# Final norm tile by tile behind the value joins, the gating join ahead of the residual's additions, and the recurrent output's spread one tile behind with two root buffers

## What is computed

```python
def rms_norm(x, g):                       # the first block's end: x = rms_norm(x, final_norm_g)
    y = xf * lax.rsqrt(jnp.mean(xf * xf, axis=-1, keepdims=True) + EPS)
    return y * g

def sgu_mixer(h, w_in, gain, w_s, b_s, w_out):
    u, v, z = jnp.split(h @ w_in, 3, axis=-1)
    u = gelu(u)
    v = rms_norm_2(gelu(v), gain)
    mixed = einsum('gpq,bcqgd->bcpgd', w_s, vc) + b_s
    return (u * mixed * silu(z)) @ w_out  # x = x + gate * this

def rwkv7_output(y, r, k_dir, v, z, r_k, ln_gain, ln_bias, w_out):
    mean = jnp.mean(yh, axis=-1, keepdims=True)                  # over each head's 64 columns
    var = jnp.mean(jnp.square(yh - mean), axis=-1, keepdims=True)
    yn = ((yh - mean) * lax.rsqrt(var + RWKV_LN_EPS)).reshape(y.shape) * ln_gain + ln_bias
    return ((yn + bonus) * silu(z)) @ w_out
```

## Time and profile before

| | |
|---|---|
| median of 3 runs | 4689.03 us (4688.02 to 4695.07) |
| profiled execution | 4691.61 us, its span 4689.6 us |
| TensorE busy | 4518.3 us, 96% of the span |
| VectorE, ScalarE, GpSimd busy | 41%, 24%, 21% |
| mean granted TensorE clock | 0.985 of full |
| chain that ended last | TensorE 89%, VectorE 6%, ScalarE 2%, issue 2% |

### The profile page before, as it was taken

One profiled execution on the slowest core, in us unless ns is written; L12 is line 12 of the kernel. 1 busy time (PEld: TensorE's weight loads), 2 busy tenths in 40 slices (PEclk: granted clock), 3 DMA queues, 4 the chain that ended last, 5 costly groups with the idle time before them and its releaser, 6 DMA issues.

```text
span 4689.6 us, 68532 instructions
## 1 busy us (share of the span) xinstructions
PE 4518.3 (96%) x29082; PEld 3061.3 (65%) x29082; DVE 1914.1 (41%) x3500; ACT 1116.1 (24%) x2249; POOL 998.9 (21%) x722
## 2 busy tenths in 40 slices
PE   9999999999999999999999989988999999999999
PEld 4446888544688887665555567776544555556888
DVE  3633452463355232224524258785201444421324
ACT  2141000113110022110423134443112333322220
POOL 1102443110244332323023000000000101003444
PEclk9999999998999999999999999999999999999999
DMA  3161222115122212111244332222111000012221
GB/s 130 54 225 63 90 95 86 47 63 216 63 90 95 86 36 72 54 54 46 105 139 151 111 86 66 81 79 101 65 69 38 30 15 30 29 54 72 95 80 69
DMA packets 115101, 378.72 MB, mean 81 GB/s; under 512 B 32752, under 2 KB 58480, under 8 KB 85360
## 3 DMA queue, kind: packets, MB, share of 16 engines
q1 hardware_dynamic: 103840, 332.92, 20.5%
q0 software_dynamic: 9808, 37.75, 2.4%
q10 hardware_dynamic: 1152, 3.67, 0.2%
HBM read 334.46 MB, written 39.85 MB: 80 GB/s over the span
## 4 chain that ended last, share of the span: by engine, by line
PE 89%; DVE 6%; ACT 2%; issue 2%; POOL 0%; DMA 0%; DVEq 0%; SPq 0%; ACTq 0%
PE ps L369 37%; PE ps L337 16%; PE ps L612 15%; PE ps L4190 2%; PE ps L2541 2%; PE ps L343 2%; PE ps L633 2%; PE ps L4109 1%; PE ps L1079 1%; PE ps L1035 1%; PE ps L4201 1%; PE ps L3195 1%; PE ps L4112 1%; PE ps L4108 1%; PE ps L4110 1%
## 5 line engine op out<-in xcount | busy, mean ns | idle before, releaser
L369 PE MATMUL ps<-A 128*128 128x256 f32 (+1 forms) x3568 | 872.0, 397 | 5.2 <-DVE A L1710 2.2
L369 PE MATMUL ps<-A,W 128*128 128x256 f32 (+1 forms) x3296 | 830.5, 405 | 5.5 <-DVE A L2398 3.1
L369 PEld LDWEIGHTS ps<-A 128*128 128x128 f32 x3568 | 676.0, 190 | 162.0 <-issue 8.5
L369 PEld LDWEIGHTS ps<-A,W 128*128 128x128 f32 x3296 | 624.6, 190 | 175.0 <-DVE A L2398 3.5
L612 PE MATMUL ps<-A,W 128*128 128x512 f32 (+1 forms) x1632 | 702.0, 585 | 2.8 <-DVE A L580 1.3
L612 PEld LDWEIGHTS ps<-A,W 128*128 128x128 f32 x1632 | 308.9, 192 | 358.4 <-issue 349.5
L337 PEld LDWEIGHTS ps<-A 64*64 64x64 f32 (+2 forms) x8032 | 379.3, 144 | 140.4 <-issue 79.2
L337 PE MATMUL ps<-A 64*64 64x64 f32 (+5 forms) x8032 | 429.7, 240 | 40.7 <-ACT A L3411 14.1
L337 PE MATMUL ps<-A,W 64*64 64x64 f32 (+3 forms) x2560 | 355.7, 322 | 8.3 <-ACT A L4356 5.8
L337 PEld LDWEIGHTS ps<-A,W 64*64 64x64 f32 (+2 forms) x2560 | 217.3, 156 | 138.7 <-issue 118.6
L440 POOL TENSOR_TENSOR A<-W 128x512 f32<-128x512 f32 (+2 forms) x88 | 133.0, 1512 | 425.8 <-PE ps L369 386.5
(11 more groups left out here) (449 smaller groups left out, 5533.2 us busy)
## 6 DMA issues: line engine op xcount, KB each, us to landing
W<-in_ada SPq DMA_DIRECT2D x48, 1024.0 KB, 5.3
W<-in_w_up SPq DMA_DIRECT2D x44, 1024.0 KB, 4.8
W<-in_w_in SPq DMA_DIRECT2D x18, 1024.0 KB, 4.8
W<-in_sgu_v SPq DMA_DIRECT2D x16, 1024.0 KB, 4.9
W<-in_sgu_u SPq DMA_DIRECT2D x16, 1024.0 KB, 4.9
W<-in_sgu_z SPq DMA_DIRECT2D x16, 1024.0 KB, 4.8
W<-in_sgu_o SPq DMA_DIRECT2D x16, 1024.0 KB, 4.8
W<-in_rw_in SPq DMA_DIRECT2D x16, 1024.0 KB, 5.1
```

Source lines behind the costliest of these rows:

```text
L369: t = e.matmul(ps, x(k), y(k), start=first and k == 0, stop=k == kt - 1, skip_group_check=True)
```

## The change

1. **Final norm.** `final_normed_dve` takes a tile number. The eight multiplications stand one each behind the joins of blocks (1, 1) to (3, 2), and the spread's bank is now always bank 5; the value blocks (1, 0) to (3, 2) of layer 0 take their banks from the other seven.
2. **Gating join.** For pair 0 of the SGU output (layers 0 and 3) the join 22, v = v + D, stands ahead of the additions of q to the residual.
3. **Recurrent output.** The root is one ScalarE instruction from PSUM with scale and bias, so that L3890 goes; it writes one of two buffers `b.rows`. P runs two tiles behind C and T four (before, one and three). The root stands ahead of the next square on ScalarE, whose table for roots is loaded before the stage. On VectorE bonus and z gate of a tile stand behind its own multiplication.
4. A spread of the MLA stage takes bank 4 in place of its turn in the ring.

```diff
-def final_normed_dve(pl, e):
-    S_, at = pl.S, ("rs", "final", SC)
+def final_normed_dve(pl, e, k):
+    S_, at, r = pl.S, ("rs", "final", SC), pl.R[:, k, SC:N]
     e.wait_ge(*S_.squares_summed.at(at))
-    for k in range(8):
-        r = pl.R[:, k, SC:N]
-        e.scalar_tensor_tensor(out=r, in0=r, scalar=vec(pl, "fg", k), in1=bank(pl, at)[:, 0:S], op0=ALU.mult,
-                               op1=ALU.mult).then_inc(*S_.normed.next(("final", k, SC), frees=at if k == 7 else None))
-    e.wait_ge(*S_.normed.last())
+    e.scalar_tensor_tensor(out=r, in0=r, scalar=vec(pl, "fg", k), in1=bank(pl, at)[:, 0:S], op0=ALU.mult,
+                           op1=ALU.mult).then_inc(*S_.normed.next(("final", k, SC), frees=at if k == 7 else None))
...
+        ring = "01234567" if i or c == 0 else "0123467"
...
-            final_spread_pe(pl, e, "final", (SC, S), 0, "latent")
+            final_spread_pe(pl, e, "final", (SC, S), 0, "latent", "5")
...
-            if (i, c, p) == (0, 1, 0):
-                final_normed_dve(pl, e)
+            if i == 0 and (c, p) > (1, 0):
+                final_normed_dve(pl, e, 3 * c + p - 4)
+    if i == 0:
+        e.wait_ge(*S_.normed.at("final", 7, SC))
...
-    add(0, b.half, q)
-    add(1, 0, q)
+    if p:
+        add(0, b.half, q)
+        add(1, 0, q)
     e.wait_ge(*S_.seventh.at(at, 7))
     e.wait_ge(*made.last())
     e.tensor_tensor(v, v, d, ALU.add).then_inc(*made.next((at, 22)))
+    if not p:
+        add(0, b.half, q)
+        add(1, 0, q)
...
-    for s in range(11):
+    for s in range(12):
         if s < 8:
             centred(s)
         if 0 <= s - 1 < 8:
             sums(s - 1)
-        if s >= 3:
-            taken_in(s - 3)
-        if 0 <= s - 1 < 8:
-            spread(s - 1)
+        if s >= 4:
+            taken_in(s - 4)
+        if 0 <= s - 2 < 8:
+            spread(s - 2)
...
 def output_act(pl, e):
+    e.activation(pl.root[:, 0:1], table(pl, "ones")[:, 0:1], ACT.Sqrt).then_inc(*S_.roots.next())
...
-        x = pl.root[:, 0:192]
-        e.wait_ge(*S_.mean_squares.at("rw_norm", k))
-        e.activation(x, x, ACT.Sqrt).then_inc(*S_.roots.next(("rw_norm", k)))
+        e.wait_ge(*S_.squares_summed.at(at))
+        if k >= 2:
+            e.wait_ge(*S_.squares_summed.at(("rw_rs", k - 2, 1)))
+        e.activation(b.rows[k % 2], bank(pl, at)[:, 0:192], ACT.Sqrt, bias=table(pl, "eps64"), scale=1.0 / 64).then_inc(
+            *S_.roots.next(at, frees=at))
...
+            x, at = b.rows[(s - 1) % 2], ("rw_norm", s - 1)
             e.wait_ge(*S_.roots.at(at))
             e.reciprocal(x, x).then_inc(*S_.inverse_roots.next(at))
+        if s < 2:
+            continue
+        k, y = s - 2, b.s_[:, s - 2, :]
+        for j, half in enumerate(b.halves):
+            at = ("rw_rs", k, j)
+            e.wait_ge(*S_.squares_summed.at(at))
+            e.scalar_tensor_tensor(out=y[:, half], in0=y[:, half], scalar=vec(pl, "lng", k), in1=bank(pl, at)[:, 0:384],
+                                   op0=ALU.mult, op1=ALU.mult).then_inc(*S_.out_normed.next(*([k] if j else []), frees=at))
+        e.wait_ge(*S_.out_normed.at(k))
+        e.wait_ge(*loads[k // 2].at("gates"))
+        e.scalar_tensor_tensor(out=y, in0=y, scalar=vec(pl, "lnb", k), in1=b.bo[:, k, :], op0=ALU.add,
+                               op1=ALU.add).then_inc(*S_.out_normed.next(("bonus", k)))
+        e.wait_ge(*S_.out_normed.at("bonus", k))
+        e.tensor_tensor(y, y, b.zz[:, k, :], ALU.mult).then_inc(*S_.z_gated.next(k))
```

More of the change, by code:

```diff
@@ L91, in constants @@
     out["sides"] = np.where(i % 32 < 16, EPS * D, EPS * EPS * D)[:, None]
+    out["eps64"] = np.full((P, 1), 64e-5)
     out["w16"] = np.stack([((i // 32) % 2 == k // 2) & (i % 2 == k % 2) for k in range(4)], 1)
@@ L216, in placed @@
     pl.MOD = ctx.enter_context(nc.sbuf_tensor("MOD", [P, 96, 2], F32))
-    pl.A_SIZE = 53202 - (8 * N + NSLOT * SLOT + n + NCOLS + 192 + 32)
+    pl.A_SIZE = 53203 - (8 * N + NSLOT * SLOT + n + NCOLS + 192 + 32)
     pl.A = ctx.enter_context(nc.sbuf_tensor("A", [P, pl.A_SIZE], F32))
@@ L2118, in values @@
         keys = {7: [("sgu_v", j, 2 * c)], 3: [("sgu_v", j, 2 * c + 1)]} if last else {}
-        return seven_pe(pl, e, at, sgu_tokens(b, p), halves_of(sgu_columns(pl, b, c), b.vt), 4, 256, "01234567", ready,
+        ring = "01234567" if i or c == 0 else "0123467"
+        return seven_pe(pl, e, at, sgu_tokens(b, p), halves_of(sgu_columns(pl, b, c), b.vt), 4, 256, ring, ready,
                         S_.first_kept.at(at), keys, bare=(i, c) == (0, 0), warmed=5 * ((i, c, p) == (3, 0, 0)))
@@ L3753, in lay_output @@
     b.s_, b.bo, b.zz = A(8, N), A(8, N), A(8, N)
+    b.rows = [A(N // 4) for _ in range(2)]
     b.x = lambda k, s: b.s_[:, k, s[0]:s[0] + s[1]]
@@ L3809, in spread @@
                     row = table(pl, "ident", o, o + 1).to_broadcast([P, 64])
-                    t = e.matmul(ps[half, 192 * c:192 * c + 192], row, pl.root[:, 0:192], start=True, stop=True)
+                    t = e.matmul(ps[half, 192 * c:192 * c + 192], row, b.rows[k % 2], start=True, stop=True)
             t.then_inc(*S_.squares_summed.next(at))
@@ L3858, in root @@
     def root(k):
[L3859 to L3861 removed]
+        at = ("rw_norm", k)
+        e.wait_ge(*S_.squares_summed.at(at))
[3 more added lines that the diff above has]
+            *S_.roots.next(at, frees=at))
     for s in range(9):
@@ L3869, in output_act @@
                     *S_.centred.next((s, j), frees=at))
-            e.wait_ge(*S_.centred.last())
+        if s:
+            root(s - 1)
+        if s < 8:
+            e.wait_ge(*S_.centred.at(s, 1))
             if s >= 2:
@@ L3873, in output_act @@
             e.activation(pl.sq[s % 2], b.s_[:, s, :], ACT.Square).then_inc(*S_.act_squares.next(("rw_norm", s)))
-        if s:
-            root(s - 1)
     end(pl, "output", "act")
@@ L3884, in output_dve @@
     for s in range(1, 10):
-        k, y = s - 1, b.s_[:, s - 1, :] if s < 9 else None
-        before = b.s_[:, s - 2, :] if s >= 2 else None
         if s < 9:
[L3888 to L3895, removed]
@@ L3896, in output_dve @@
-        if s < 9:
+            x, at = b.rows[(s - 1) % 2], ("rw_norm", s - 1)
             e.wait_ge(*S_.roots.at(at))
             e.reciprocal(x, x).then_inc(*S_.inverse_roots.next(at))
[L3899 to L3909, removed]
+        if s < 2:
+            continue
@@ L4036, in mla_pe @@
     features_pe(pl, e, "ml_cq", [("ml_cq", i) for i in range(3)], 8, 256, b.h, b.xseg, ring=wide, ready=ready, warmed=6,
-                beside=lambda m, seg: squares(m - 1) if m else spread_pe(pl, e, ("mod", 2), BOTH, order=BOTH[0:1]))
+                beside=lambda m, seg: squares(m - 1) if m else spread_pe(pl, e, ("mod", 2), BOTH, "4", order=BOTH[0:1]))
     features_pe(pl, e, "ml_ckv", ["ml_ckv"], 8, 256, b.h, b.segs, ring=wide, ready=ready,
```

## The result

The changed kernel takes 4674.83 us, the median of 7 runs (4665.76 to 4677.28); the kernel before took 4690.65 us on the same chip (7 runs, 4687.21 to 4699.22). The ratio is 0.996, with a 95% interval of 0.995 to 0.997: 15.8 us less, where 14.6 were forecast (4674.4, from the 4689.03 of the first three runs). The profiled execution took 4668.58 us, its span 4666.6 us, which is 6.3 us under the median, where the profile before stood 2.6 us above the median it was taken with.

The account below looks back on a forecast made before the run. TensorE, busy for 96% of the span, was taken as the bound, so only its waits and slow clock counted. 5.7 + 4.6 + 4.3 = 14.6 us off the median of 4689.03 gave 4674.4 us, range 4667 to 4682.

Parts of the forecast that it names:

- Final norm, 5.7 us forecast: SGU values, layer 0: a 4.05 us bank wait and its slow clock go, 6.98 us, less a new 1.3 us wait.
- the eighth tile's wait: Ahead of `sgu_u`: product 1 needs bank 5, which the norm's last tile frees, so TensorE newly waits 1.3 us.
- rival (d): SGU values: the norm wait was for VectorE and moves to the next join; first term -1.3, time 4681.4; chance 0.05.
- Rival (c): Value blocks: with seven banks, A waits for the block before's C; slower, time 4698; chance 0.05.
- its 1.1 us to spare: Value blocks: A takes the bank of the block before's C, whose freeing is hidden behind product 4 with 1.1 us over.
- Gating join, 4.6 us forecast: SGU output, layer 3: 3.09 us wait and 1.79 us slow clock go, less a 0.3 us wait for bank 0.
- Recurrent output, 4.3 us forecast: Gain at the stage's start: its end moves from 3297.7 to 3293.4, despite a new wait ahead of the fourth S.
- if the stage from the first C to the last T isn't 56 us: Recurrent output: the prediction's sign of being wrong; it expected 56 us, against 60.7 before.
- TensorE waits 4.0 us ... I take 2.3: Recurrent output, fourth S: z landing after 10.1 us delays the bonus; a 4.0 us wait plus 2.3 us slow clock.
- rival (a): Recurrent output: the bonus doesn't wait for its loads; third term 9.7 us, time 4669.0; chance 0.2.
- Rival (b): Clock falls ahead of `sgu_u` (2.9 us) and at recurrent output's start (3.7 us); gain 8.0, time 4681.0; chance 0.24.
- the third term: The recurrent output's gain, forecast at 4.3 us, between 0.6 and 9.7 us.

Follow-up runs that it names:

- x4_bank: Kernel before with only the final norm's bank choice and the MLA spread's bank 4, the eight multiplications left in one piece: 4686.43 us, ratio 0.9979.
- x2_join: Kernel before with only the gating join moved ahead of the additions of q: 4691.98 us, ratio 0.999.
- x8_first: Changed kernel with A's addition of pair 0 ahead of the two of q in the SGU output: 4672.82 us, ratio 0.9955 to the kernel before.
- x1_norm: Kernel before with only the final norm's single tiles and banks, and the MLA spread's bank 4: 4683.14 us against 4696.31, ratio 0.9973.
- after_again: The changed kernel run once more, nothing altered: 4671.67 us, ratio 0.9953 to the kernel before.
- x6_slab: Changed kernel with the first slab of output weights loaded behind tile 1's bonus and z too: 4672.23 us, ratio 0.9955 to the kernel before.
- x3_out: Kernel before with only the recurrent output's new order: 4686.99 us, ratio 0.9987.

## Why the prediction came out right, point by point

- **Final norm, 5.7 us forecast: 5.69.** The wait for a bank, its slow clock, the eighth tile's wait (1.3 forecast, 1.17 in the row, 1.44 in the stretch) and the kept clock behind it all held. `x4_bank` shows that the bank was the cause; rival (d) is wrong. Rival (c) is wrong too: a block takes 12.11 us. But the prediction's reading of the turns there, with its 1.1 us to spare, is wrong: a block takes four turns of seven, so A gets the bank of C of the block before the last, and it is D that gets the bank of the block before's A. In the profile after, ScalarE is done with A of block (1, 1) at 1720.06 and product 7 of block (1, 2) wants the bank at 1728.14: 8.1 us to spare. The rival was less likely than its working made it.
- **Gating join, 4.6 us forecast: 4.67.** `x2_join` shows it alone, `x8_first` that the 0.27 us left was bank 0. Of this term the slow clock's part (1.8) isn't the wait's fixed price: in `x1_norm` and `x4_bank` the same 3.09 us wait left the clock up, and the stretch at 49.03 us. Measured from there the edit is worth 2.98 us. That the term came out to 0.1 us is in part luck: the profile before was one of those in which the clock fell.
- **Recurrent output, 4.3 us forecast: 8.3.** This is the term that was mis-sized, and by the prediction's own sign ("if the stage from the first C to the last T isn't 56 us") it was wrong here: the stage took 52.46 us. TensorE's order of events was right to 0.1 us up to C4. Two figures of the step "TensorE waits 4.0 us ... I take 2.3" failed. z landed 8.5 us behind its issue in the place of 10.1, which made the wait 1.65 us shorter. The landing time of one execution had been carried over as if it were fixed, and that execution was the odd one: in the nine other profiles whose slab stands ahead of this z it took 8.2 to 8.9 us, in `x1_norm`, `x2_join` and `x4_bank` too, whose recurrent output is the old one. So the new order didn't make it sooner. Why it took 10.1 that once no run shows. And the clock didn't fall, 2.3 us more. 1.65 + 2.3 is the 4.0 that the term was short. In `after_again` it did fall, and the term was 6.35. So the truth lies between the forecast and rival (a): the mechanism of the forecast (the bonus waits), most of (a)'s gain. `x6_slab` is rival (a) made true: 50.29 us, 10.5 gained, where (a) had 9.7.
- **Rival (b)** doesn't hold as priced: the clock stayed up at the wait ahead of `sgu_u` in all seven profiles that have it, and at the start of the recurrent output of the five profiles with the third edit as the change has it, it fell in one (`after_again`), for 1.7 us and not 3.7.
- **The sum** came out nearer than its terms: 14.6 forecast, 18.7 in the two profiles' own stretches, 15.8 by the medians. So the agreement is in part luck: the third term was 4 us too small, and the medians show some 3 us less than the stretches of the two profiles.

## What to carry to other kernels

A wait for a PSUM bank can look like a wait for the work that happens to free it. Ask which event the wait is on; giving that bank a turn of its own got 5.36 of 5.7 us without moving any work. When a pipeline is deepened, look for the load that the old order hid, and price its landing from more than one trace and from the order of the queue: here one profile had it 1.6 us too late, and the loads' order was worth another 2.2 us. For changes worth a few us in 4700, cut the traces at the same instructions and compare stretches; the total hides them.

## What the runs showed of the hardware that was not expected

The granted clock's fall behind a wait is no fixed price. In the three changed places it fell behind 4.05 us (in three profiles of three), behind the 4.12 us of the old recurrent output (in four of four) and behind 3.64 us (once); behind 3.09 us it fell in two profiles (before and `x3_out`, 50.72 us) and stayed up in two (`x1_norm` and `x4_bank`, 49.03); behind 2.60 and 2.62 us it fell once and stayed up once; behind 2.35, 2.07 and 1.17 us it stayed. But a short wait doesn't keep it up everywhere: behind the waits of 1.02 and 0.69 us in the MLA stage it fell in three of the fourteen profiles (before, `after_again`, `x6_slab`). Where it fell it cost 1.7 us behind the waits of 2.60, 3.09 and 3.64 us and in the MLA stage, and 2.9 behind 4.05. What decided between equal waits no run here shows. The pair at 3.09 us, product 4 of pair 0 in the timelines of `x1_norm` and `x3_out`, which run the same instructions there:

```profile
4602.74 3.72 PE L369 MATMUL ps<-A,W 128*128 128x256 f32 x16 [3.09 <-DVE A L2398]
```

```profile
4602.14 5.41 PE L370 MATMUL ps<-A,W 128*128 128x256 f32 x16 [3.09 <-DVE A L2399]
```

The changed kernel's stretch with the features and the scan, which has many waits of 1 to 2.5 us and some up to 4.7, took 1415.05 us in one execution and 1418.66 in another, and the stretch to layer 3's output was either 1290.7 or 1292.3 us in every profile.
